# Expert 30's down weights and products ahead of expert 31's gate and up, at the end of a 32-expert decoder step

## The reference, cut to what matters

```python
def expert_block(args):
    tok, e = args
    xb = x2[tok]
    gu = xb @ w_gate_up[e] + b_gate_up[e]
    gt = jnp.minimum(gu[:, :D_FF], SWIGLU_LIMIT)
    up = jnp.clip(gu[:, D_FF:], -SWIGLU_LIMIT, SWIGLU_LIMIT)
    glu = gt * jax.nn.sigmoid(gt * SWIGLU_ALPHA)
    return ((up + 1.0) * glu) @ w_down[e] + b_down[e]
...
contrib = y_rows[dest] * sorted_gate[:, None].astype(y_rows.dtype)
return jnp.zeros_like(x2).at[sorted_tok].add(contrib).reshape(shp)
```

## Time and profile before

| | us |
|---|---|
| median of three runs | 1262.3 |
| the profiled execution | 1261.57 |
| its span, first to last instruction | 1259.7 |
| PE busy in it | 1202.0 (95%) |
| DVE busy | 415.8 (33%) |
| ACT busy | 233.9 (19%) |
| SP's weight queue busy, as a share of the 16 DMA engines | 96.7% |

### The profile page before, as it was taken

How to read it: one execution, slowest core, us unless ns; L and a number is a source line. 1 busy time by engine, 2 the same in 40 slices (tenths; PEclk the granted TensorE clock), 3 DMA queues, 4 the chain that set the end, 5 groups by cost and what they waited for, 6 DMA issues and landing times.

```text
span 1259.7 us, 14690 instructions
## 1 busy us (share of the span) xinstructions
PE 1202.0 (95%) x6122; PEld 516.4 (41%) x6122; DVE 415.8 (33%) x917; ACT 233.9 (19%) x459; POOL 74.7 (6%) x79
## 2 busy tenths in 40 slices
PE   9999999899999999999998999999999899999986
PEld 4456678675533333333333333333333333333322
DVE  3275654335531322213232222213131323222233
ACT  2212433130211210111111010111011121101112
POOL 0353003300200000000000000000000000000000
PEclk9999999999999999999999999999999999999999
DMA  9999999999799999999999999999999999999994
GB/s 342 391 307 367 338 358 342 303 320 424 267 403 431 425 438 430 430 432 432 430 432 429 432 432 431 431 431 428 432 430 431 432 430 430 432 433 425 429 426 163
DMA packets 64712, 502.36 MB, mean 399 GB/s; under 512 B 5872, under 2 KB 30064, under 8 KB 48112
## 3 DMA queue, kind: packets, MB, share of 16 engines
q1 hardware_dynamic: 62784, 497.10, 96.7%
q0 software_dynamic: 848, 2.36, 0.6%
q10 hardware_dynamic: 1008, 1.90, 0.4%
HBM read 498.42 MB, written 37.03 MB: 425 GB/s over the span
## 4 chain that ended last, share of the span: by engine, by line
PE 66%; DMA 28%; DVE 3%; SPq 1%; issue 1%; ACT 0%; DVEq 0%; ACTq 0%
DMA ring<-in_w_gate_up 21%; PE ps L1902 21%; PE ps L1945 13%; PE ps L1268 6%; PE ps L1354 5%; PE ps L1861 3%; PE ps L1799 3%; DMA low<-in_w_gate_up 3%; DMA high<-in_w_gate_up 3%; PE ps L1649 2%; PE ps L1662 2%; PE ps L1921 1%; PE ps L1818 1%; PE ps L1330 1%; PE ps L1400 1%
## 5 line engine op out<-in xcount | busy, mean ns | idle before, releaser
L1902 PE MATMUL ps<-ring,high 128*64 128x512 f32 x1216 | 272.3, 595 | 21.1 <-DMA ring<-in_w_gate_up 21.1
L1902 PEld LDWEIGHTS ps<-ring,high 128*64 128x64 f32 x1216 | 86.2, 136 | 184.6 <-issue 155.1
L1945 PE MATMUL ps<-ring,high 128*64 128x512 f32 x608 | 138.1, 596 | 0.7 <-issue 0.7
L1354 PE MATMUL ps<-low,ring 128*128 128x288 f32 x384 | 102.0, 412 | 0.0
L1150 ACT ACTIVATE high<-ps 128x512 f32<-128x512 f32 x32 | 19.1, 597 | 442.0 <-PE ps L1921 442.0
L1902 PE MATMUL ps<-high 128*64 128x512 f32 x416 | 93.4, 595 | 6.9 <-DMA high<-in_w_gate_up 6.9
L1902 PE MATMUL ps<-low,high 128*64 128x512 f32 x416 | 93.0, 595 | 5.1 <-DMA low<-in_w_gate_up 5.1
L2443 DVE TENSOR_REDUCE low<-ps 128x1 f32<-128x288 f32 x15 | 6.9, 458 | 274.1 <-PE ps L1831 274.1
L1354 PEld LDWEIGHTS ps<-low,ring 128*128 128x128 f32 x384 | 69.7, 190 | 22.0 <-issue 5.2
L1945 PEld LDWEIGHTS ps<-ring,high 128*64 128x64 f32 x608 | 42.5, 136 | 75.3 <-issue 72.1
L2471 DVE TENSOR_TENSOR x_tok<-x_tok,ps 64x512 f32<-64x512 f32 (+2 forms) x48 | 41.3, 860 | 76.6 <-PE ps L1861 74.1
(11 more groups left out here) (381 smaller groups left out, 1203.9 us busy)
## 6 DMA issues: line engine op xcount, KB each, us to landing
ring<-in_w_gate_up SPq DMA_DIRECT2D x28, 4096.0 KB, 37.7
ring<-in_w_down SPq DMA_DIRECT2D x14, 4096.0 KB, 39.9
ring<-in_w_gate_up SPq DMA_DIRECT2D x20, 2048.0 KB, 21.5
high<-in_w_gate_up SPq DMA_DIRECT2D x10, 4096.0 KB, 37.7
low<-in_w_gate_up SPq DMA_DIRECT2D x9, 4096.0 KB, 38.2
ring<-in_w_down SPq DMA_DIRECT2D x10, 2048.0 KB, 19.3
low<-in_w_down SPq DMA_DIRECT2D x5, 4096.0 KB, 37.9
high<-in_w_down SPq DMA_DIRECT2D x5, 4096.0 KB, 39.4
```

What stands on the lines that cost most here:

```text
L1354: ins = pe.matmul(gate_out(m), wblk[AREA[6 + m // 4]][:, k, (m % 4) * P:(m % 4 + 1) * P], hT_v[:, k, :], start=(k == 0), stop=(k == KC - 1))
L1902: ins = pe.matmul(bank(gu0 + u)[64 * h:64 * h + 64, :], xTe[:, k % 4, (k // 4) * 64:(k // 4) * 64 + 64], every_other_four(pair_buf[slot][: ...
L1945: ins = pe.matmul(bank(7 if last else 5)[64 * h:64 * h + 64, :], aT[:, kk % 4, (kk // 4) * 64:(kk // 4) * 64 + 64], pair_buf[slot][:, a:a ...
```

## The change

In the list of weight pieces, expert 30's two down pieces go ahead of expert 31's four gate and up pieces: pieces 184 and 185 are now `down(30)`, 186 to 189 are `gate_up(31)`. 190 and 191 stay.

On PE the loop ends with b = 30. After it come `a_transposes(30)`, the whole of `down(30)`, `gate_up(31)`, `sel_transposes(16)`, `a_transposes(31)` and `down(31)`. Inside `gate_up(31)` the spread of pair 15 stands behind slices 0, 1 and 3 in place of 3, 4 and 6, and its second part (banks 4 and 5) waits for ACT to have copied the result of `down(30)` out of bank 5. On DVE, `activate(30)` goes from behind `split_rows(15)` to ahead of it, and the entries of the spread matrix for experts 30 and 31 are built ahead of `add_rows(15)`. On ACT, `gate_sigmoid(30)` and `evict_at(30)` go ahead of `split_rows(15)`, `evict_y(30)` goes ahead of the work on expert 31, and `evict_selt(16)` ahead of `evict_at(31)`.

```diff
@@ -461,7 +461,8 @@
         stream = [("g", 0, k) for k in range(4)]
         for e in range(1, NE):
-            stream += [("g", e, k) for k in range(4)] + [("d", e - 1, j) for j in range(2)]
+            ups, downs = [("g", e, k) for k in range(4)], [("d", e - 1, j) for j in range(2)]
+            stream += ups + downs if e < NE - 1 else downs + ups
         stream += [("d", NE - 1, j) for j in range(2)]
...
+        SCATTER_AT = (3, 4, 6), (0, 1, 3)
@@ -1194,23 +1196,26 @@
-            for b in range(1, NE):
+            for b in range(1, NE - 1):
                 gate_sigmoid(b - 1)
                 if b == 1:
                     evict_selt(0)
                 evict_at(b - 1)
-                if b + 1 < NE:
-                    evict_rows(b + 1)
-                else:
+                evict_rows(b + 1)
+                if b == NE - 2:
                     gate_sigmoid(b)
+                evict_y(b - 1, (b - 1) // 2, (b - 1) % 2)
+                if b == NE - 2:
                     evict_at(b)
-                    evict_selt(NPAIR)
-                evict_y(b - 1, (b - 1) // 2, (b - 1) % 2)
                 if b % 2 == 0:
                     split_rows(b // 2)
...
+            evict_y(NE - 2, NPAIR - 1, 0)
+            gate_sigmoid(NE - 1)
+            evict_selt(NPAIR)
+            evict_at(NE - 1)
             evict_y(NE - 1, NPAIR - 1, 1)
@@ -1845,6 +1850,8 @@
                 elif t == 0 and sc_bank(n, 2) == sc_bank(n, 0):
                     pe.wait_ge(S["sc_added"], 3 * n + 1)
+                elif t == 1 and isinstance(n, int) and n == NPAIR - 1:
+                    pe.wait_ge(S["y_evicted"], 2 * (NE - 1))
@@ -1907,8 +1914,8 @@
-                        elif b > 1 and k in (3, 4, 6):
-                            scatter(b // 2, SC_ORDER[(3, 4, 6).index(k)])
+                        elif b > 1 and k in SCATTER_AT[b == NE - 1]:
+                            scatter(b // 2, SC_ORDER[SCATTER_AT[b == NE - 1].index(k)])
@@ -1963,27 +1970,27 @@
-            for b in range(1, NE):
+            for b in range(1, NE - 1):
                 gate_up(b, 2 * (b % 2), expert_hot(b))
                 if b % 2 == 1 and b > 1:
                     pe.wait_ge(S["sc_added"], 3 * (b // 2) + 2)
                 a_transposes(b - 1)
-                if b + 1 < NE:
-                    if b % 2 == 1 and b > 1:
-                        pe.wait_ge(S["sc_added"], 3 * (b // 2) + 3)
-                    gather(b + 1)
+                if b % 2 == 1 and b > 1:
+                    pe.wait_ge(S["sc_added"], 3 * (b // 2) + 3)
+                gather(b + 1)
                 down(b - 1, 0, 2)
                 if b % 2 == 0:
                     sel_transposes(b // 2)
-                if b + 1 < NE:
-                    x_transposes(b + 1)
-                else:
-                    a_transposes(b)
-                    sel_transposes(NPAIR)
+                x_transposes(b + 1)
                 down(b - 1, 2, 4)
...
+            a_transposes(NE - 2)
+            down(NE - 2, 0, 4)
+            gate_up(NE - 1, 2 * ((NE - 1) % 2), expert_hot(NE - 1))
+            sel_transposes(NPAIR)
+            a_transposes(NE - 1)
             down(NE - 1, 0, 4)
@@ -2473,21 +2480,25 @@
             for b in range(1, NE):
                 if b % 2 == 1 and b > 1:
                     split_rows(b // 2)
-                activate(b - 1, 2 * ((b - 1) % 2), link)
-                if b + 1 < NE and b >= 1:
+                if b + 1 < NE:
+                    activate(b - 1, 2 * ((b - 1) % 2), link)
                     expert_row(b + 1)
+                else:
+                    gate_select_block(NE - 2)
+                    gate_select_block(NE - 1)
                 if b % 2 == 1 and b > 1:
                     add_rows(b // 2)
-                gate_select_block(b - 1)
                 if b + 1 < NE:
+                    gate_select_block(b - 1)
                     select(b + 1)
                     if b % 2 == 0:
                         evict_selt(b // 2)
                     evict_x(b + 1)
+                if b == NE - 2:
+                    activate(b, 2 * (b % 2), link)
...
             activate(NE - 1, 2 * ((NE - 1) % 2), link)
-            gate_select_block(NE - 1)
```

## The result

The changed kernel takes 1266.88 us (median of six runs, 1264.39 to 1269.25); the kernel before took 1264.19 us on the same chip (six runs, 1261.93 to 1266.19). The two medians lie 2.7 us apart; the ratio is 1.0025, with a 95% interval from 1.0013 to 1.0037: slower by 1.6 to 4.7 us. On a second chip the ratio was 1.0041 (1.0028 to 1.0055), slower by 3.5 to 6.9 us; the medians there were 1267.31 and 1261.97 us. The forecast was +3.0 us on a level of 1262.3; the level itself was 1.9 us higher in six runs than in the three shown, and the time lies just above the range.

The account below looks back on a forecast made before the run. Bound: the landing of piece 186 and 26.8 us of PE work behind it. Gaps after 1216.52 grow from 0.73 to 3.45 us (+2.7), differently split work adds 0.3: +3.0, median 1265.3 us, range 1262.9 to 1266.8.

Parts of the forecast that it names:

- The level: Whole kernel: the same +3.0 us put on the median of the kernel before, giving 1265.3 us.
- the +3.6 that the forecast allowed: End of down(31): upper bound on the slowdown, with piece 189 landing 0.6 us later than by the trace.
- The landings: Weight stream: landings keep their times by position, 185 at 1211.6, 186 at 1216.5, 189 at 1231.2 us.
- one landing may have been late in this execution alone: Wait between slices 0 and 2, cited for the transfers rival (chance 0.10); kernel before could end up to 0.5 us sooner.
- The activation of 31: Between gate_up(31) and down(31): PE waits out a 4.40 us chain, working 1.2 and idling 3.2 us.
- The clock: Rival: in the new gap PE falls to 1.2 GHz, down(31) takes 14.1 us, +10 in all, 1272.4; chance 0.04.
- The wait for the copies of `down(30)`: Ahead of the scatter behind slice 1, about 1221 us: ACT has finished by then, so no cost.
- The waits for `activate(30)` and `evict_at(30)`: Ahead of down(30): 1.4 us in all, costing nothing because the wait for piece 185 swallows them.
- The early spread: Scatters of pair 15 inside gate_up(31), 0.76, 1.40 and 1.40 us, counted as PE work with split_rows(15) ready in time.
- the tail behind `down(31)`: Copies, f32 spread, adds, norm and output after down(31): the same, at the same cost.

Follow-up runs that it names:

- the short filling: Changed kernel plus 5 idle products ahead of the transposes of expert 31's activation and 1 ahead of down(31); ratio 1.0029 to the kernel before.

## Why the prediction missed, point by point

**The level.** The step that failed first is "I put the same +3.0 on the median: 1265.3 us", with a range that allowed 0.9 us for the scatter of the runs. Three runs gave 1262.3 as the level before; six gave 1264.19, and fifteen on each of two other chips 1261.97 and 1262.14. In three traces of the unchanged kernel the last stretch begins at 1200.27, 1204.61 and 1200.36 us. A range for an absolute time has to carry that, some 2 us to either side of a median of three; only the difference can be held closer. The sign of the difference held, and on this chip its size: +3.0 forecast, 1.0025 measured, which is +3.2 on 1264.19. On the second chip 1.0041 is +5.2, above the +3.6 that the forecast allowed. That the size came out on the first chip is luck, as the points below show.

**The landings.** "I take the landings by position as they are" holds for piece 186, which slice 4 of `gate_up(31)` waits for with the old order and slice 0 with the new one. Where it is on time, that slice starts 14.7 us behind the transposes with the old order (1215.09 - 1200.36) and 14.6 to 15.0 with the new one; where it is late, 15.9 and 16.3 with the old and 16.2 and 16.4 with the new. The Trainium skill (DMA: Bandwidth & Descriptors, section "Queues, rings and completion order") has each DMA engine take a ring's descriptors in order. These landings by position agree with it. But the values of the forecast came from an execution in which piece 185 and all behind it were late: 185 took 43.2 us from issue to landing there, and 41.6 in the third trace of the unchanged kernel. In the late traces of the new order (the third of the changed kernel and the first with the short filling) 185 took 41.6 too, and only 186 and what follows are late. The profiled changed kernel had them on time: slice 0 14.8 us behind the transposes where the forecast had 16.3, and `gate_up(31)` ended after 1234.23 - 1201.20 = 33.0 us where it had 34.6. That term was 1.6 us too long. The forecast itself named the possibility ("one landing may have been late in this execution alone"), but allowed the kernel before a gain of only 0.5 us by it, where its stretch was 1.6 us shorter with the landings on time (41.5 against 43.1). So it compared with an execution whose stretch was itself 1.6 us long. What makes a landing late I don't know; no run separates it.

**The activation of 31.** "This is the term that decides" was right. The chain from the end of `gate_up(31)` to the start of `down(31)` was forecast at 4.40 us; it measured 4.27, 4.28 and 4.57 in the three traces. PE idled 2.30 + 0.69 us in it, forecast 3.2.

**The clock.** This rival, at a chance of 0.04 and a price of +7 us, is where the reasoning failed. The sum had the clock's term at nothing. The fall came in every trace in which the gap was left empty, the three of the changed kernel and that with the spread put back; what was wrong in the price is that the low clock lasts only a few us and costs 1.4 to 2.7 us (8.47, 8.78 and 9.73 against 7.06), not the whole of `down(31)`. The evidence against it was one row: after 2.60 us idle at 1211.63 the clock held. One stretch that held says little about the next: single waits of 2.07 and 2.52 us brought the clock down elsewhere, the first in the unchanged kernel itself, and one of 2.54 did not. Here two stretches stood close together, 2.30 and 0.69 us with four transposes between them; whether the second one matters no run tells. The Trainium skill (TensorE: Matmul & The Clock Gate, section "HAM oscillation — how this bites in real kernels") describes a kernel whose clock falls at every long wait for data between bursts of products. The traces agree that waits between bursts can bring the clock down. They show it for a wait of 2.07 us, shorter than those of that kernel, and here the measurement decides.

**How the errors met.** From the transposes to the end of `down(31)` the forecast had 34.6 + 4.4 + 7.1 = 46.1 us. Measured were 33.0 + 4.3 + 8.5 = 45.8. The landings, 1.6 us too late, and the clock that was left out, 1.4, nearly cancel. Against a kernel before in the same state of landings, the change costs 4.3 to 6.0 us in this stretch, and not 3.0. The timed runs have it at 3.2 on one chip and 5.2 on the other; how many of them had late landings is not on record.

**The other points.** The wait for the copies of `down(30)` held nobody: scatter tile 1 follows slice 1 without a gap for ACT. The waits for `activate(30)` and `evict_at(30)` (1.29 us) are most likely free, as forecast, since slice 0 waits for its weights behind them; what swallows them is that wait and not one for piece 185, which no trace of the changed kernel has. No run takes them out. The early spread, taken as free, is worth 1.8 to 2.1 us. No term of the tail behind `down(31)` moved: the last f32 spread starts 0.9 us behind `down(31)` in both.

A version that beats both was not found. The one with half of `down(30)` behind `gate_up(31)` comes level with the kernel before, and its `down(31)` waits for weights; by the times of the earlier trace rows and the prediction (1241.05 and 1236.1) the last half of piece 191 lands 4.9 us behind piece 190 and needs 1.8 us of products, so an estimate is that `down(31)`, 7.1 us long, could end at most 0.4 us sooner behind the landing of piece 190.

## What to carry to other kernels

A hand-ordered pipeline that runs products of one item beside the activation of another should not be reordered for the sake of the loads before it is clear that every activation keeps products beside it; here the last one was stripped of them. Price a new idle stretch of PE at its length and at the clock it may lose. Keep real work beside the wait first (half of `down(30)` gave back 4.2 us of the stretch); small independent products that only fill the gap gave back 0.9 to 1.3. Compare two traces from a common event behind which only the change differs, and trace the same program two or three times before trusting a landing time to 1 us.

## What the runs showed of the hardware

- The granted clock fell to 0.50 (1.2 GHz) in each of four traces around idle stretches of 2.30 and 0.69 us with 0.75 to 1.03 us of transposes between them, and was back at 1.00 before `down(31)` ended. It held at 1.00 behind single stretches of 2.60 and 2.39 us in the kernel before and of 2.54 us in the changed one, and fell behind single stretches of 2.07 us (kernel before) and 2.52 us. Behind two stretches of 1.29 and 1.96 us, with 7.5 us of products between them, it fell; behind 1.29 and 1.79 us, in another trace, it held.
- Ten idle f32 matmul instructions in the first stretch and two in the second went with a clock of 1.00 in both traces, and so did twenty and four in a third.
- Two executions of one program differed by 1.6 us in how long a weight piece took from issue to landing (43.2 and 41.6) and by 4 us in when the last stretch began (1204.61 and 1200.36).
